# The shared rotary key of the latent attention, projected by four column groups and summed by stacked identities

## The chip, the cores and the metric

The kernel runs on one core of a Trainium2 chip. The metric is the device time of one execution in microseconds; lower is better. Below, TensorE is the matrix engine (PE in the profile; PEld are its weight loads), VectorE is DVE, ScalarE is ACT, GpSimd is POOL, and SyncE (SP) issues most of the large transfers.

## The reference, cut to what matters

Two layers of a transformer-like block work on 256 latent tokens and 256 context tokens of width 1024. In each layer the normed and modulated rows `h` are multiplied by one wide matrix `w_in`, whose 1952 columns hold the inputs of four groups of mixing heads. Columns 384 to 415 are the rotary key `kr`, 32 numbers for each token, shared by the four heads of the latent attention:

```python
zx = hx @ w_in[layer]
zc = hc @ w_in[layer]
...
_, ckv, kr, _, bk, bv, _, dk, dv, _ = split_in(z)
k_rope = kr.reshape(B, L, 1, MLA_ROPE)
if ropes is not None:
    k_rope = apply_rope(k_rope, rope_a)
ka = jnp.concatenate([k_nope, jnp.broadcast_to(k_rope, (B, L, MLA_HEADS, MLA_ROPE))], axis=-1)
```

The rotation is applied to the latent tokens alone. After mixing, each layer runs a mixture of 16 experts. Everything is float32.

## The kernel before, in words

Each engine has its own instruction list, written out by hand and joined by semaphores (`mark` counts one up, `at` gives the value to wait for). Activations lie transposed in `hT`, as 8 slices of 128 rows of the width by 512 tokens (256 latent, then 256 context).

**Projection (`project`, TensorE, L508 to L569).** The columns of `w_in` come in four chunks, loaded by SyncE into three staging buffers. The tiles are made in the order `cq0`, `cq1`, `ckv`, `kr`; `bk`, `bv`, `bq0`, `bq1`; `dq0`, `dk0`, `dq1`, `dk1`; `dv0`, `dv1`, `u0`, `u1`. A tile is a sum over the 8 slices of the width, that is 8 matmuls into one PSUM bank. `take` hands out six banks in a ring and waits until what last lay in the bank was read. For `kr` each of the 8 matmuls has 32 output partitions (64 to 95 of the bank). In layer 1 the first chunk is done differently: `cq0` and `cq1` for the latent tokens, then the transposes that make the context half of `hT`, then `ckv` and `kr` for tokens 0 to 255 and `ckv` and `kr` for tokens 256 to 511, with 256 columns to a matmul. Behind `bk` stand the sums of squares of `cq` (`square_part`, L482), behind `bq1` those of `ckv`. In layer 0, behind the second, third and fourth chunk, a piece of the modulation product stands (`ada_item`, L496): 8 matmuls of 32 output partitions, over four column groups of TensorE.

**What reads the tiles (ScalarE, `project`, L1096 on).** ScalarE copies the tiles out of PSUM in the same order: `cq0`, `cq1`, their squares, `ckv`, `kr` (32 rows, L1106, into `kr[64:96]` in the buffer `lat`), `bk`, then the inverse norm of `cq`, and so on. In layer 0 it first issues the constants' load and small weights' loads (`rest_of_loads`, L1345 on).

**The rotation.** `rotate` (L571) multiplies the copied tile by a matrix that swaps and negates halves. For `kr` this uses 32 rows and 32 columns of `rot_mla`. GpSimd multiplies the tile by the cosines, VectorE the rotated one by the sines, adds both (`rope`), and copies the result to the four heads' keys (L1449). The rotations are the first step after the projection (`latent_projections`, L579), with a wait there for the constants.

`va`, the values of the latent attention, has a buffer of 128 x 1024 in `W[0]` that stays unused until the end of `latent_projections`.

Of the kernel before, what the change touches and what calls it, by code (L numbers as in the profile page):

```python
# [23 lines left out]
P = 128  # L24
D = 1024
KD = D // P
SEQ = 256
# [31 lines left out]
def constants():  # L59
# [45 lines left out]
    put("inv_count", inv_count.reshape(P, -1))  # L105

# [58 lines left out]
def hybrid_block(nc, A, out, known=None):  # L165
    ctx = ExitStack()
    with ctx:
# [54 lines left out]
        qas, kas, bqs, bks, dqs, dks, vas, bvs, dvs, dgs = places.values()  # L222

# [235 lines left out]
        def _(pe):  # L459
# [48 lines left out]
            def project(L):  # L508
                S, nq = f"pe_in{L}", q_tokens(L)

                def tile(name, w, t, lo, hi):

                    col, _ = TILES[name]
                    m, p0 = (MLA_ROPE, MLA_NOPE) if name == "kr" else (P, 0)
                    for k in range(KD):
                        if name in ("cq0", "ckv"):
                            for s in range(lo // SEQ, hi // SEQ):
                                pe.wait_ge(*at("h", L, s, k))
                        if name in ("bq0", "bq1"):

                            for b in range(2):
                                c0 = b * P + int(name[2]) * 64
                                mm = nc.tensor.matmul(t[64 * b:64 * b + 64, lo:hi], w[:, k, c0:c0 + 64], hT[:, k, lo:hi],  # L523
                                                      start=(k == 0), stop=(k == KD - 1), skip_group_check=True)
                        else:
                            mm = nc.tensor.matmul(t[p0:p0 + m, lo:hi], w[:, k, col:col + m], hT[:, k, lo:hi],  # L526
                                                  start=(k == 0), stop=(k == KD - 1))
                    return mm

                for c, names in enumerate((("cq0", "cq1", "ckv", "kr"), ("bk", "bv", "bq0", "bq1"),  # L530
# [17 lines left out]
                    for name in names:  # L548
# [15 lines left out]
                        if name == "bk":  # L564
                            for j in range(2):
                                square_part(S, ("cq", L), j, 2, sq[j][:, 0:nq])
# [3 lines left out]
            def rotate(S, L, name, x, kind, lo, hi):  # L570
# [3 lines left out]
                r = C("rot_" + kind)  # L574
                nc.tensor.matmul(t[lo:hi, 0:SEQ], r[lo:hi, lo:hi], x, start=True, stop=True)\  # L575
                    .then_inc(*mark(S, ("filled", "rot", L, name)))
# [457 lines left out]
        def _(act):  # L1034
# [61 lines left out]
            def project(L):  # L1096
# [9 lines left out]
                copy(S, kr[64:96, :], ("kr", L), lo=64, hi=96, keys=[("tile", L, "kr")])  # L1106
                copy(S, bks[L], ("bk", L), keys=[("tile", L, "bk")])
                finish_rstd(S, ("cq", L), 1, (0, nq), 256, ("ckvn", L - 1) if L else None)
# [1085 lines left out]
```

## Time and profile before

| | us |
|---|---|
| median of 3 executions | 1181.54 (1181.15 to 1188.02) |
| the profiled execution | 1180.66 |
| its span, first to last instruction | 1178.8 |
| TensorE busy | 989.8 (84%) |
| VectorE, ScalarE, GpSimd busy | 314.3, 264.3, 189.6 |
| projection of layer 0 | 34 to about 140 |
| experts of layer 0 | about 430 to 660 |
| projection of layer 1 | 700 to 797 |
| experts of layer 1 | about 930 to 1166 |

Times are counted from the first instruction. An engine's list is worked through in order; a timeline's bracket gives the idle time ahead of a row and what ended it. Each fp32 matmul stands as two records (`x16` is 8 matmuls), and its weight load as two. The weight load of a pass is done while the pass before it runs, so the distance between starts of weight loads gives the pace. The chain of waits is followed back from the last instruction of the kernel.

### The profile page before, as it was taken

The numbers are of one execution on the slowest core, as the hardware profiler recorded it, in microseconds if no ns is written. First come the engines' busy times: TensorE is split into PE (matmuls) and PEld (weight loads), VectorE is DVE, ScalarE is ACT, GpSimd is POOL, SyncE is SP. The second block draws the span as 40 slices with busy tenths as digits, with TensorE's granted clock in tenths as the row PEclk, the third lists the DMA queues.
The fourth block names the chain that finished last, engine by engine and source line by source line (L and its number), as shares of the span: only waits on it lengthen the run. The fifth ranks groups of instructions, "written<-read, shape, count | busy, mean of one in ns | idle before, by whom it ended". The sixth has DMA issues, their size and how long they took to land. (4 is left out here: it accounts for less than half of the span.)

```text
span 1178.8 us, 24765 instructions
## 1 busy us (share of the span) xinstructions
PE 989.8 (84%) x9688; PEld 608.8 (52%) x9689; DVE 314.3 (27%) x876; ACT 264.3 (22%) x708; POOL 189.6 (16%) x312
## 2 busy tenths in 40 slices
PE   3999999999999398987899438999998668798776
PEld 2354646555555365654566235676654444455443
DVE  1100045446632611111111060006562501111112
ACT  4121024445433100100111142114553100000002
POOL 0010015000013211211112110003202222222211
PEclk9999999999999599999999759999999689999899
DMA  9973527765453698999989951320107888999992
GB/s 377 342 223 141 214 90 271 283 241 224 144 232 107 249 377 354 414 424 426 381 335 421 409 207 31 112 72 1 38 1 272 375 353 354 415 414 367 430 428 92
DMA packets 56423, 313.64 MB, mean 266 GB/s; under 512 B 12282, under 2 KB 20516, under 8 KB 37796
## 3 DMA queue, kind: packets, MB, share of 16 engines
q1 hardware_dynamic: 36480, 280.00, 58.9%
q0 software_dynamic: 7152, 24.58, 6.0%
q10 hardware_dynamic: 12724, 8.11, 2.2%
q8 instruction: 49, 0.80, 0.3%
q14 instruction: 18, 0.15, 0.0%
HBM read 304.21 MB, written 14.75 MB: 271 GB/s over the span
## 5 line engine op out<-in xcount | busy, mean ns | idle before, releaser
L914 PE MATMUL psum<-weights,lat 128*32 128x256 f32 x2688 | 165.5, 399 | 41.5 <-issue 21.7
L914 PEld LDWEIGHTS psum<-weights,lat 128*32 128x32 f32 x2688 | 102.9, 115 | 100.4 <-issue 63.7
L526 PE MATMUL psum<-hT,weights 128*128 128x512 f32 (+3 forms) x384 | 137.3, 518 | 4.7 <-ACT lat L1094 3.2
L526 PEld LDWEIGHTS psum<-hT,weights 128*128 128x128 f32 (+1 forms) x384 | 71.1, 187 | 68.4 <-issue 55.3
L929 PE MATMUL psum<-weights,lat 128*32 128x256 f32 x1344 | 82.2, 382 | 5.4 <-ACT lat L1265 5.3
L1256 ACT ACTIVATE lat<-psum 128x128 f32<-128x128 f32 x64 | 17.7, 277 | 289.3 <-PE psum L914 249.7
L1478 DVE TENSOR_REDUCE st<-psum 128x1 f32<-128x512 f32 (+1 forms) x96 | 55.9, 598 | 72.3 <-PE psum L651 26.2
L688 PE MATMUL psum<-weights,R 128*128 128x64 f32 x480 | 63.3, 271 | 5.5 <-ACT R L1171 4.1
L914 PE MATMUL psum<-hT,lat 128*32 128x256 f32 x672 | 46.3, 419 | 25.2 <-issue 14.3
L1158 ACT ACTIVATE R<-psum,st 128x512 f32<-128x512 f32 (+1 forms) x78 | 48.0, 615 | 83.9 <-DVE st L1478 40.0
L929 PEld LDWEIGHTS psum<-weights,lat 128*32 128x32 f32 x1344 | 51.0, 110 | 29.0 <-issue 9.5
L688 PEld LDWEIGHTS psum<-weights,R 128*128 128x128 f32 x480 | 59.2, 191 | 9.7 <-ACT R L1171 9.0
L770 PE MATMUL psum<-weights,hT 128*128 128x512 f32 x144 | 63.5, 595 | 0.2 <-ACT hT L1195 0.2
L1717 DVE STREAM_TRANSPOSE lat<-psum 128x256 f32<-128x256 f32 x25 | 11.3, 450 | 190.0 <-PE psum L853 186.5
L1724 DVE STREAM_TRANSPOSE lat<-lat 128x256 f32<-128x256 f32 x41 | 18.3, 446 | 145.9 <-PE psum L914 140.4
L2007 POOL TENSOR_SCALAR x_tok<-x_tok 128x256 f32<-128x256 f32 x23 | 28.3, 1232 | 166.4 <-PE psum L899 166.0
L1094 ACT ACTIVATE weights<-psum 128x512 f32<-128x512 f32 (+4 forms) x40 | 22.1, 552 | 128.6 <-PE psum L526 55.2
L914 PEld LDWEIGHTS psum<-hT,lat 128*32 128x32 f32 x672 | 25.4, 118 | 43.3 <-issue 36.4
L496 PE MATMUL psum<-weights,silu_c 128*32 128x512 f32 x384 | 46.0, 598 | 1.3 <-DMA weights<-in_ada_w_dram 1.3
L2041 POOL DMA_INDIRECT lat<-h_rows,slot_col x42 | 41.2, 981 | 33.1 <-POOL slot_col L2038 32.3
L1886 POOL TENSOR_TENSOR R<-weights,cst 128x256 f32<-128x256 f32 (+1 forms) x22 | 14.9, 676 | 181.4 <-DVE lat L1435 138.5
L914 PE MATMUL psum<-R,lat 128*32 128x256 f32 x672 | 42.6, 391 | 1.6 <-DMA R<-in_exp_w_gu_dram 1.6
(290 smaller groups left out, 1299.9 us busy)
## 6 DMA issues: line engine op xcount, KB each, us to landing
weights<-in_exp_w_gu_dram SPq DMA_DIRECT2D x44, 2048.0 KB, 12.0
weights<-in_ada_w_dram SPq DMA_DIRECT2D x24, 2048.0 KB, 7.8
weights<-in_exp_w_down_dram SPq DMA_DIRECT2D x22, 2048.0 KB
hT<-in_exp_w_gu_dram SPq DMA_DIRECT2D x10, 2048.0 KB
R<-in_exp_w_gu_dram SPq DMA_DIRECT2D x10, 2048.0 KB
spare_w<-in_exp_w_down_dram SPq DMA_DIRECT2D x10, 2048.0 KB
weights<-in_w_in_dram SPq DMA_DIRECT2D x6, 2048.0 KB, 24.2
weights<-in_w_out_dram SPq DMA_DIRECT2D x4, 2048.0 KB, 8.1
```

The source lines that it names most:

```text
L496: mm = nc.tensor.matmul(psum[32 * g:32 * g + 32, B_ADA, :], silu_c[:, k, :], w[:, k2, g, :], start=(k == 0), stop=(k == 7), skip_group_che ...
L526: mm = nc.tensor.matmul(t[p0:p0 + m, lo:hi], w[:, k, col:col + m], hT[:, k, lo:hi], start=(k == 0), stop=(k == KD - 1))
L688: mm = nc.tensor.matmul(t[:, 0:64], probT[u % 2][:, i, :], v, start=(i == 0), stop=(i == n - 1))
L770: nc.tensor.matmul(t, mixT[:, k, tt * P:(tt + 1) * P], w[:, k, :], start=(k == 0), stop=False)
L914: mm = nc.tensor.matmul(gu_ps[BLK * j:BLK * j + BLK, 0:256], (xgT if L < LAST else xgT_last)[:, k, :], w[:, k % 4, j, :, :], start=(k == 0 ...
L929: mm = nc.tensor.matmul(y_ps[BLK * j:BLK * j + BLK, 0:256], actT[:, b, :], w_dn[place][:, b, j * 256:(j + 1) * 256], start=(b == 0), stop= ...
L1094: a(dst, src, ACT.Copy, scale=scale).then_inc(*mark(S, ("read", *job), *keys))
L1158: a((prob[u % (AHEAD + 1)] if v == 0 else prob2)[:, 0:nk], read(act, "s", L, u, v)[:, 0:nk], ACT.Exp, bias=s_[:, v:v + 1], accum_out=s_[:, ...
L1478: ins = red(s_[:, j:j + 1], read(v, "s", L, u, j)[:, 0:nk], AX.X, ALU.max, negate=True)
L1724: nc.vector.transpose(xgT[:, :, :].rearrange("p k s -> p (k s)"), xg[par]).then_inc(x_ready, 1)
L2007: nc.gpsimd.tensor_scalar(hot, tokens, pair_col[:, 0:1], pair_col[:, 1:2], ALU.is_equal, ALU.mult).then_inc(sem("hot_ready"), 1)
L2041: g_.indirect_dma_start(xg[par], None, h_parts, bass.IndirectOffsetOnAxis(ap=slot_col[:, par:par + 1], axis=0))\
```

## The change

`kr`'s eight matmuls go to four groups of 32 output partitions: slice k of the width to group k mod 4, so that each group sums two slices. The four partial tiles fill all 128 partitions of the bank. ScalarE copies them whole into `kr_parts`, which lies in the unused buffer of `va`. A new step `sum_kr` on TensorE, behind `bk`, multiplies them by four stacked 32x32 identities, which adds the four parts; its result goes to partitions 64 to 95 of another bank, and a second copy of ScalarE, behind that of `bk`, brings it to where the key lay before. The rotation reads the partial tiles, with the rotation stacked four times. The constants grow by two matrices of 32 columns.

```diff
+    put("sum_kr", np.tile(np.eye(MLA_ROPE), (QUADS, 1)))
+    put("sum_rot_kr", np.tile(rot_kr, (QUADS, 1)))
...
+        kr_parts = vas[0].rearrange("p t c -> p (t c)")[:, 0:NTOK]
...
+                        elif name == "kr":
+
+                            p0 = MLA_ROPE * (k % 4)
+                            mm = nc.tensor.matmul(t[p0:p0 + MLA_ROPE, lo:hi], w[:, k, col:col + MLA_ROPE], hT[:, k, lo:hi],
+                                                  start=(k < 4), stop=(k >= 4), skip_group_check=True)
...
+                def sum_kr():
+
+                    pe.wait_ge(*at("const"))
+                    t = take("kr_sum", L)
+                    pe.wait_ge(*at("read", "kr", L))
+                    nc.tensor.matmul(t[MLA_NOPE:MLA_QK, :], C("sum_kr"), kr_parts, start=True, stop=True).then_inc(*mark(S, ("filled", "kr_sum", L)))
...
                         if name == "bk":
+                            sum_kr()
                             for j in range(2):
...
+                if name == "kr":
+                    mm = nc.tensor.matmul(t[lo:hi, 0:SEQ], C("sum_rot_kr"), kr_parts[:, 0:SEQ], start=True, stop=True)
...
-                copy(S, kr[64:96, :], ("kr", L), lo=64, hi=96, keys=[("tile", L, "kr")])
+                copy(S, kr_parts, ("kr", L))
                 copy(S, bks[L], ("bk", L), keys=[("tile", L, "bk")])
+                copy(S, kr[64:96, :], ("kr_sum", L), lo=64, hi=96, keys=[("tile", L, "kr")])
```

TensorE, layer 0, from `kr` to `bv`. Names stand for buffers: `hT` the activations, `weights` the staged matrix or the mixing buffers, `spare_w` the squares; in brackets the semaphores waited for (`act_in0` counts ScalarE's copies of this projection). Before:

```order
L526 MATMUL psum<-hT,weights 32x512 [waits act_start]
L526 MATMUL psum<-hT,weights 32x512 x7
L526 MATMUL psum<-hT,weights 128x512 [waits v_start,dma_stage4]
L526 MATMUL psum<-hT,weights 128x512 x7
L482 MATMUL psum<-spare_w,ones 128x512 [waits act_in0] x2
L556 MATMUL psum<-weights,hT 128x128 [waits v_start]
```

And of the change:

```order
L534 MATMUL psum<-hT,weights 32x512 [waits act_start]
L534 MATMUL psum<-hT,weights 32x512 x7
L537 MATMUL psum<-hT,weights 128x512 [waits v_start,dma_stage4]
L537 MATMUL psum<-hT,weights 128x512 x7
L546 MATMUL psum<-weights,cst 32x512 [waits act_in0,v_start,dma_const]
L489 MATMUL psum<-spare_w,ones 128x512 [waits act_in0] x2
L574 MATMUL psum<-weights,hT 128x128 [waits act_in0]
```

The eight matmuls of `kr` keep their place and number. Between `bk` and the squares stands the product with the identities, with waits for a copy of ScalarE and for the constants; the first matmul of `bv` behind them waits for one of ScalarE's copies too.

ScalarE, layer 0, from the last small loads to the copy of the squares' sum (L1050 before, L1072 in the change). Before:

```order
L1358 DMA subln<-in_diff_subln_dram 128x64
L1094 ACTIVATE lat<-psum 128x512 [waits pe_in0] x2
L1042 ACTIVATE spare_w<-lat 128x512 [waits act_in0] x2
L1094 ACTIVATE lat<-psum 128x512 [waits pe_in0]
L1094 ACTIVATE lat<-psum 32x512 [waits pe_in0]
L1094 ACTIVATE weights<-psum 128x512 [waits pe_in0]
L1050 ACTIVATE spare_w<-psum,cst 128x512 [waits pe_in0]
```

And of the change:

```order
L1381 DMA subln<-in_diff_subln_dram 128x64
L1116 ACTIVATE lat<-psum 128x512 [waits pe_in0] x2
L1064 ACTIVATE spare_w<-lat 128x512 [waits act_in0] x2
L1116 ACTIVATE lat<-psum 128x512 [waits pe_in0]
L1116 ACTIVATE weights<-psum 128x512 [waits pe_in0] x2
L1116 ACTIVATE lat<-psum 32x512 [waits pe_in0]
L1072 ACTIVATE spare_w<-psum,cst 128x512 [waits pe_in0]
```

The 32-row copy into `lat` has moved behind the copy of `bk`, and a full copy of the partial tiles stands where it was.

## Rows read from the trace of the kernel before

**Rows 1.** The page: busy time of each engine, share of the span, instructions.
```profile
PE 989.8 (84%) x9688; PEld 608.8 (52%) x9689; DVE 314.3 (27%) x876; ACT 264.3 (22%) x708; POOL 189.6 (16%) x312
```

**Rows 2.** Timeline of TensorE, layer 0: start, length, line, out<-in, count, idle before.
```profile
33.99 36.45 PE L526 MATMUL psum<-hT,weights 128*128 128x512 f32 x80 [1.52 <-DVE hT L1855]
...
95.94 14.32 PE L526 MATMUL psum<-hT,weights 128*128 128x512 f32 x33
```

**Rows 3.** Chain of waits, layer 1: start, length, what.
```profile
716.36 23.23 PE psum L526 x80
...
797.08 2.04 PE psum L575 x8
```

**Rows 4.** Timeline of TensorE's weight loads around the key, layer 0, columns as above.
```profile
56.32 0.14 PEld L526 LDWEIGHTS psum<-hT,weights 128*32 128x32 f32 x2 [0.76 <-issue]
...
57.21 0.11 PEld L526 LDWEIGHTS psum<-hT,weights 128*32 128x32 f32 x1 [0.32 <-issue]
57.64 0.11 PEld L526 LDWEIGHTS psum<-hT,weights 128*32 128x32 f32 x1 [0.32 <-issue]
...
63.31 0.30 PEld L526 LDWEIGHTS psum<-hT,weights 128*128 128x128 f32 x2 [0.84 <-issue]
```

**Rows 5.** The same view around the key's two halves, layer 1.
```profile
716.33 5.00 PEld L526 LDWEIGHTS psum<-hT,weights 128*128 128x128 f32 x16 [3.39 <-ACT lat L1094]
721.67 3.16 PEld L526 LDWEIGHTS psum<-hT,weights 128*32 128x32 f32 x16 [0.33 <-issue]
725.24 3.32 PEld L526 LDWEIGHTS psum<-hT,weights 128*128 128x128 f32 x16 [0.41 <-issue]
728.89 3.16 PEld L526 LDWEIGHTS psum<-hT,weights 128*32 128x32 f32 x16 [0.33 <-issue]
732.46 0.30 PEld L526 LDWEIGHTS psum<-hT,weights 128*128 128x128 f32 x2 [0.41 <-issue]
```

**Rows 6.** Windows: length, busy of PE, PEld, DVE, ACT, POOL, granted clock, DMA share, GB/s.
```profile
60.00:65.00 5.00, 5.00 (x12) 1.53 (x11) 0.00 (x0) 3.19 (x6) 0.00 (x0) 1.00 0.25 39
443.00:650.00 207.00, 177.08 (x3116) 118.36 (x3111) 35.72 (x99) 21.49 (x66) 38.29 (x66) 0.99 0.96 394
718.00:720.00 2.00, 2.00 (x6) 1.56 (x6) 0.00 (x0) 0.00 (x0) 0.00 (x0) 0.55 0.00 0
720.00:722.00 2.00, 2.00 (x11) 1.41 (x10) 0.00 (x0) 0.00 (x0) 0.00 (x0) 1.00 0.00 0
```

**Rows 7.** Timeline of weight loads around a modulation piece in four column groups.
```profile
93.12 0.16 PEld L496 LDWEIGHTS psum<-weights,silu_c 128*32 128x32 f32 x8 [0.81 <-issue]
...
94.97 0.30 PEld L482 LDWEIGHTS psum<-spare_w,ones 128*128 128x128 f32 x2 [0.84 <-issue]
```

**Rows 8.** Chain of waits, an expert's first product in four column groups.
```profile
937.59 3.59 PE psum L914 x64
```

**Rows 9.** Timeline of weight loads around the key's rotation, layer 1.
```profile
797.01 0.13 PEld L575 LDWEIGHTS psum<-lat,cst 32*32 32x32 f32 x2 [0.33 <-issue]
797.55 1.16 PEld L575 LDWEIGHTS psum<-weights,cst 128*128 128x128 f32 x6 [0.41 <-ACT up L1127]
```

**Rows 10.** Timeline of ScalarE and of its queue (ACTq), layer 0.
```profile
43.92 11.49 ACTq L455 DMA_DIRECT2D w_pool<-in_pool_w_dram  x4
...
60.66 1.08 ACT L1094 ACTIVATE lat<-psum 128x512 f32<-128x512 f32 x2 [23.48 <-issue]
...
63.42 0.59 ACT L1094 ACTIVATE lat<-psum 32x512 f32<-32x512 f32 x1 [0.15 <-PE psum L526]
70.48 0.60 ACT L1094 ACTIVATE weights<-psum 128x512 f32<-128x512 f32 x1 [6.48 <-PE psum L526]
```

**Rows 11.** Issues of DMA at 5.29, 33.28 and 63.41 us: KB, us to landing.
```profile
weights<-in_w_in_dram SPq DMA_DIRECT2D x1, 2048.0 KB, 38.6
cst<-in_constants_dram ACTq DMA_DIRECT2D x1, 1631.5 KB, 10.5
weights<-in_w_in_dram SPq DMA_DIRECT2D x1, 2048.0 KB, 7.9
```

More of the change, by code:

```diff
@@ L105, in constants @@
     put("inv_count", inv_count.reshape(P, -1))
+    rot_kr = rot(MLA_ROPE, MLA_NOPE, MLA_QK)[MLA_NOPE:MLA_QK, MLA_NOPE:MLA_QK]
+    put("sum_kr", np.tile(np.eye(MLA_ROPE), (QUADS, 1)))
+    put("sum_rot_kr", np.tile(rot_kr, (QUADS, 1)))
     put("before", np.triu(np.ones((P, P)), 1) - 1.0)
@@ L513, in tile @@
                     col, _ = TILES[name]
-                    m, p0 = (MLA_ROPE, MLA_NOPE) if name == "kr" else (P, 0)
                     for k in range(KD):
@@ L524, in tile @@
                                                       start=(k == 0), stop=(k == KD - 1), skip_group_check=True)
+                        elif name == "kr":
+                            p0 = MLA_ROPE * (k % 4)
+                            mm = nc.tensor.matmul(t[p0:p0 + MLA_ROPE, lo:hi], w[:, k, col:col + MLA_ROPE], hT[:, k, lo:hi],
+                                                  start=(k < 4), stop=(k >= 4), skip_group_check=True)
                         else:
-                            mm = nc.tensor.matmul(t[p0:p0 + m, lo:hi], w[:, k, col:col + m], hT[:, k, lo:hi],
+                            mm = nc.tensor.matmul(t[:, lo:hi], w[:, k, col:col + P], hT[:, k, lo:hi],
                                                   start=(k == 0), stop=(k == KD - 1))
                     return mm
+                def sum_kr():
[3 more added lines that the diff above has]
+                    nc.tensor.matmul(t[MLA_NOPE:MLA_QK, :], C("sum_kr"), kr_parts, start=True, stop=True).then_inc(*mark(S, ("filled", "kr_sum", L)))
                 for c, names in enumerate((("cq0", "cq1", "ckv", "kr"), ("bk", "bv", "bq0", "bq1"),
@@ L573, in rotate @@
                 t = take("rot", L, name)
-                r = C("rot_" + kind)
-                nc.tensor.matmul(t[lo:hi, 0:SEQ], r[lo:hi, lo:hi], x, start=True, stop=True)\
-                    .then_inc(*mark(S, ("filled", "rot", L, name)))
+                if name == "kr":
+                    mm = nc.tensor.matmul(t[lo:hi, 0:SEQ], C("sum_rot_kr"), kr_parts[:, 0:SEQ], start=True, stop=True)
+                else:
+                    r = C("rot_" + kind)
+                    mm = nc.tensor.matmul(t[lo:hi, 0:SEQ], r[lo:hi, lo:hi], x, start=True, stop=True)
+                mm.then_inc(*mark(S, ("filled", "rot", L, name)))
             def latent_projections(L):
```

## The prediction

> **What bounds the kernel now.** I read the page first, then the granted clock, the chain of waits, and the timelines of each engine around the two places where the rotary key is projected. The page [rows 1] shows TensorE busy for 989.8 us, 84% of the span of 1178.8 us. The execution's own time is 1180.66 us, so 1.9 us lie outside the span. The question is whether TensorE sets the pace just where the change sits. It does in both layers. In layer 0 the timeline of TensorE [rows 2] runs from 33.99 us to 110 us; its seven rows, of which the first and the last stand there, have an idle entry at the first alone. In layer 1 the chain of waits [rows 3] is TensorE's own work from 716.36 us on, through the whole projection to the rotations (L575, 797.08 us): nine rows, of which the first and the last stand there. Nothing else ends last there, so each microsecond taken off TensorE in the projection comes off the span, unless something not timed by TensorE then ends later.
>
> **What is removed.** In layer 0 the key takes 8 matmuls of 32 output partitions by 512 tokens. Each fp32 matmul has two records. The rows of the weight loads [rows 4] show its 16 passes: the first load starts at 56.32 us, the first load of the tile behind it (`bk`) at 63.31 us, so the piece costs 63.31 - 56.32 = 6.99 us. Sixteen passes at the spacing of 0.43 us (57.21 to 57.64 us) are 6.86 us; 0.13 us is what going into and out of the narrow shape costs. In layer 1 the key is made in two halves of 256 tokens, 16 passes each: 721.67 to 725.24 us and 728.89 to 732.46 us [rows 5], 3.57 us each, 7.14 us together. Removed in all: 14.13 us. The granted clock is 1.00 where layer 1's first half begins [rows 6], the level of 2.4 GHz, and 512 columns in 0.43 us in layer 0 are the same pace as 16 passes of 256 in 3.57 us, so these prices are full-speed ones.
>
> **What takes its place.** The eight slices of the width now go to four column groups of 32 output partitions, two slices to each. The trace has this very shape: a piece of the modulation product (L496, 128*32, 512 columns, 8 matmuls over four groups, also all into one bank). Its first load is at 93.12 us and the next line's at 94.97 us [rows 7]: 1.85 us for 16 passes, against 6.99 us for the same number now. That is four passes of 0.43 us plus the same 0.13 us. For 256 columns the nearest row is the expert product (L914), 64 passes in 3.59 us [rows 8], so 16 passes in 0.90 us; with the entry and exit cost 0.13 us I take 1.0 us for each half. New: 1.85 + 2 x 1.0 = 3.85 us. Saved: 14.13 - 3.85 = 10.3 us.
>
> **What is added.** One matmul with the stacked identities per layer (512 columns, 32 output partitions, so two passes of 0.43 us) plus 0.13 us for entering and leaving the shape: 1.0 us. The trace's nearest row is the rotation of this key, one 256-column matmul between wide ones: 797.01 to 797.55 us [rows 9], 0.54 us, which is 0.43 us of passes and 0.11 us besides, so the estimate holds for that as well. Two layers: 2.0 us. The rotation itself keeps its columns and only contracts over 128 rows instead of 32; the passes are counted in columns (16 passes of `ckv`, 128 output partitions, start 3.65 us before the key's next ones, which take 3.57 us with 32 [rows 5]), so I take zero. The sum: -10.3 + 2.0 = **-8.3 us**.
>
> **What is added elsewhere, at nothing.** ScalarE copies a full 128x512 tile instead of 32x512 (0.60 and 0.59 us [rows 10]), and has one more copy of 0.6 us per layer. It idles 6.48 us before the `bk` copy [rows 10], and behind it waits for the square sums, two matmuls of 0.86 us; the new copy (about 66.3 to 66.9 us in the shifted layer 0) fits before these are ready at about 68 us. Without that cover it would cost 0.6 us a layer, 1.2 us. The constants grow by 64 columns, 32 KB on a 1631.5 KB load: 0.08 us at 394 GB/s [rows 6]. They land at 33.28 + 10.5 = 43.8 us [rows 11], long before the sum's matmul at about 65 us. More takes from the bank ring make later tiles wait for newer reads, but in the order only `bv`'s first matmul gets such a wait, for a copy (`cq0`) done by 61.7 us [rows 10].
>
> **What must come earlier with TensorE.** `bk` would start at 58.2 us instead of 63.3. Its weights were issued at 5.29 us and took 38.6 us: 43.9 us [rows 11]. The last chunk is issued when the first is used (63.41 us, landing 7.9 us later [rows 11]), so it moves along. The same holds for the modulation weights and expert weights further on: they are issued as TensorE releases buffers. The DMA queues are nearly saturated in the experts, at a share of 0.96 over 207 us [rows 6], but that stretch starts relative to TensorE too.
>
> **The tightest new wait.** Queued behind the sum's matmul on TensorE are the square sums, then `bv` and all else. It waits for ScalarE's copy of the four partial tiles. ScalarE cannot begin its projection copies before 60.66 us, as it is issuing small loads until then [rows 10]. Then come two copies, two squares and the `ckv` copy; it was free for the key at 63.42 - 0.15 = 63.27 us, so the partial tiles are copied by 63.9 us. TensorE finishes `bk` at about 65.1 us (ScalarE's copy of it began at 70.48 us, so it ended at about 70.3 us, less 5.1). The margin is 1.2 us. In layer 1 it is over 6 us: the partial tiles are full at about 727.3 us and `bk` lasts seven more.
>
> **Rivals.**
> 1. *The wait on ScalarE decides* (the one that ends slower). ScalarE's issues once took long: four small loads 11.49 us, to 55.4 us [rows 10], while weight loads filled the DMA queues; the ten behind them took 5.2 us. The last weight chunk is now issued at 58.3 us, inside ScalarE's last issues. Were these stretched by x, TensorE would stall x - 1.2 us; beyond x = 9.5 us the gain is gone, and a repeat of 11.49 us gives a stall of 10.3 us and 1183.5 us. Against it: the transfer needs a while to flow (before, it was issued at 63.41 us and the DMA share of 60 to 65 us is 0.25 [rows 6, 11]), by which time ScalarE is done. 3 in 100. The Trainium skill (TensorEngine Tiling (Array Packing), Performance Considerations) warns of this kind of bound: tiling speeds up TensorE but not the copies out of PSUM. By that rule ScalarE would set the pace here; the rows of this stretch show it idle before each copy instead.
> 2. *The column groups overlap less well.* If the groups reading the same activations did not overlap at all, nothing is saved and 2.0 us is added: 1183.5 us. L496 and L914 speak against it [rows 7, 8], both with all groups reading the same partitions. 3 in 100. The Trainium skill (TensorE: Matmul & The Clock Gate, Part 3) gives 2.38x measured for three column groups and 3.07x for four row groups, less than the 3.8x that 6.99 / 1.85 makes here; by 3.07x the new piece would be 14.13 / 3.07 = 4.6 us and the sum -7.5 us. The sum above goes by the trace.
> 3. *The clock's slow stretches fall otherwise.* After TensorE's pause before 716.33 us (3.39 us) the clock is at 0.55 in 718 to 720 us, mostly its level of 1.2 GHz, and at 1.00 behind that; those first 16 passes take 5.34 us instead of the 3.65 of the next wide ones [rows 5, 6]: 1.7 us. All work behind shifts by 4 to 8 us, and the experts have many pauses. One such stretch more or less is 1.7 us; two or three more in one direction make 1178 or 1168 us. 12 in 100 for a result over 3.5 us off the sum, either side.
>
> **How the numbers follow.** The profiled execution predicts 1180.66 - 8.3 = 1172.4 us. It lay 0.9 us below the median of 1181.54 us, so the median should be 1181.54 - 8.3 = **1173.2 us**. The forecast has 82 in 100, in 1170 to 1177 us. Rivals 1 and 2 at 1183.5 us together have 6. A range of 1168.5 to 1179 us takes in the clock cases and a partly stretched ScalarE, and leaves out about 1 in 10. A measurement of this kernel can tell about 1% (11.8 us) from no change. Faster by more than that needs a time under 1169.7 us, beyond the 10.3 us removed without any new cost: 6 in 100, by clock stretches only. Slower by over 1% (above 1193 us) needs a stall beyond rival 1's price: 2 in 100. Within 1%: 92.
>
> **What the new profile would show.** Right: weight loads of the key's matmuls in a burst of about 1.85 us in layer 0 and 1.0 us twice in layer 1; `bk` loads starting near 58.2 us; a 128*32 matmul from the constants of about 0.9 us behind `bk`, with no idle time in front; every later row of layer 0 up to the experts about 4.1 us earlier, the second layer's end about 8.3. Wrong: an idle entry of TensorE at the sum, released by ScalarE; key passes spaced by 0.43 us; or an offset between the traces that shrinks in the experts.

## The result, and the profile of the changed kernel

The changed kernel took 1172.68 us (median of 7 executions, 1168.27 to 1176.79), the kernel before 1184.85 us (7, 1181.15 to 1188.02). The ratio is 0.9901, with a 95% interval of 0.9875 to 0.9928: 11.7 us less, 8.5 to 14.8. (Here and below the times are medians. The ratio is worked out from all executions and is not that of the medians; a difference is the ratio times the median of the kernel before.) The forecast was 1173.2 us and 8.3 us less. The time lay in the range. The difference was larger than forecast, and the first question is whether the missing 3.4 us belong to the change.

The profiled execution took 1168.27 us. Its page, in the parts that answer to [rows 1] and to the clock:

```profile
span 1166.4 us, 24777 instructions
PE 975.9 (84%) x9692; PEld 604.2 (52%) x9693; DVE 313.7 (27%) x876; ACT 266.0 (23%) x710; POOL 189.6 (16%) x312
PEclk9999999989999699999999859999999689999988
q8 instruction: 49, 0.80, 0.3%
```

TensorE is busy for 13.9 us less than in [rows 1], at the same share of the span, with four records more (two passes of the sum in each layer). ScalarE has two more instructions and 1.7 us more work. The mean granted clock is 0.947, against 0.941 before. The last line, packets that bring instructions, looked like nothing at first. It matters below.

The timeline of TensorE's weight loads, layer 0 and then layer 1, columns as in [rows 4]:

```profile
54.78 0.16 PEld L534 LDWEIGHTS psum<-hT,weights 128*32 128x32 f32 x8 [0.76 <-issue]
55.23 0.13 PEld L534 LDWEIGHTS psum<-hT,weights 128*32 128x32 f32 x4 [0.30 <-issue]
55.66 0.13 PEld L534 LDWEIGHTS psum<-hT,weights 128*32 128x32 f32 x4 [0.30 <-issue]
56.63 0.30 PEld L537 LDWEIGHTS psum<-hT,weights 128*128 128x128 f32 x2 [0.84 <-issue]
...
717.28 0.59 PEld L534 LDWEIGHTS psum<-hT,weights 128*32 128x32 f32 x16 [0.33 <-issue]
718.28 3.32 PEld L537 LDWEIGHTS psum<-hT,weights 128*128 128x128 f32 x16 [0.41 <-issue]
721.93 0.59 PEld L534 LDWEIGHTS psum<-hT,weights 128*32 128x32 f32 x16 [0.33 <-issue]
722.93 0.30 PEld L537 LDWEIGHTS psum<-hT,weights 128*128 128x128 f32 x2 [0.41 <-issue]
...
729.99 0.14 PEld L546 LDWEIGHTS psum<-weights,cst 128*32 128x32 f32 x2 [0.76 <-issue]
730.97 0.73 PEld L489 LDWEIGHTS psum<-spare_w,ones 128*128 128x128 f32 x4 [0.84 <-issue]
```

In layer 0 the key's sixteen passes go from 54.78 us to the next tile's first load at 56.63 us: 1.85 us, where [rows 4] have 6.99. The loads come in three bursts (8, 4 and 4), one for each pass time of 0.43 us. In layer 1 the halves take 718.28 - 717.28 = 1.00 us and 722.93 - 721.93 = 1.00 us, against 3.57 us in [rows 5]. The sum takes 730.97 - 729.99 = 0.98 us. Each of these is the forecast's own figure within 0.02 us.

What was not forecast stands in the timeline of TensorE, layer 0, to be read with [rows 2]:

```profile
34.01 20.84 PE L537 MATMUL psum<-hT,weights 128*128 128x512 f32 x48 [1.52 <-DVE hT L1878]
54.78 1.92 PE L534 MATMUL psum<-hT,weights 128*32 128x512 f32 x16
56.63 7.13 PE L537 MATMUL psum<-hT,weights 128*128 128x512 f32 x16
64.78 1.02 PE L546 MATMUL psum<-weights,cst 128*32 128x512 f32 x2 [1.02 <-ACT weights L1116]
65.73 1.98 PE L489 MATMUL psum<-spare_w,ones 128*128 128x512 f32 x4
```

and in ScalarE's timeline, the rows that answer to [rows 10]:

```profile
43.99 11.55 ACTq L462 DMA_DIRECT2D w_pool<-in_pool_w_dram  x4
...
58.29 0.68 ACTq L1381 DMA_DIRECT2D rt_b<-in_router_gb_dram  x1
...
61.55 1.08 ACT L1116 ACTIVATE lat<-psum 128x512 f32<-128x512 f32 x2 [24.34 <-issue]
...
64.03 1.09 ACT L1116 ACTIVATE weights<-psum 128x512 f32<-128x512 f32 x2
```

TensorE stands still for 1.02 us ahead of the sum, released by ScalarE's copy (L1116). That is rival 1 on a small scale, and it works against the change. The first of the two copies in the last row is that of the partial tiles. ScalarE starts its copies at 61.55 us instead of 60.66, and TensorE gets to the sum at 64.78 - 1.02 = 63.76 us instead of the forecast 65.1.

So the gain beyond the forecast came from elsewhere. The table sets the start of the same weight loads, issued by SyncE as TensorE releases their buffers, beside each other in both traces:

| issue (place) | before | after | difference |
|---|---|---|---|
| fourth chunk of the projection, layer 0 | 63.41 | 56.77 | -6.64 |
| first modulation weights behind it | 95.10 | 90.66 | -4.44 |
| output projection, layer 0 | 297.61 | 296.33 | -1.28 |
| first projection chunk, layer 1 | 645.37 | 641.13 | -4.24 |
| fourth chunk, layer 1 | 732.56 | 723.06 | -9.50 |
| first expert weights, layer 1 | 890.21 | 881.88 | -8.33 |
| span | 1178.8 | 1166.4 | -12.4 |

Where the change sits the steps are as forecast: layer 1 gains 5.26 us between the fourth and fifth rows (5.14 forecast), then gives back the sum. In layer 0 the -6.64 us is 5.14 us of the change and 1.5 us of an earlier start. Elsewhere the difference wanders over stretches that the change doesn't touch: by 3.2 us between the second and third rows, by 3.0 us between the third and fourth, and by 4.1 us behind the last issue. The windows view says why; the columns are those of [rows 6], first the kernel before and then the changed one:

```profile
34.00:38.00 4.00, 4.00 (x6) 1.84 (x7) 1.81 (x6) 3.18 (x7) 0.00 (x0) 0.61 1.07 405
250.00:265.00 15.00, 14.89 (x93) 8.05 (x92) 6.46 (x29) 5.58 (x22) 1.72 (x3) 1.00 0.74 274
```

```profile
34.00:38.00 4.00, 3.99 (x10) 1.85 (x11) 1.83 (x6) 3.21 (x7) 0.00 (x0) 1.00 1.09 410
250.00:265.00 15.00, 15.00 (x69) 7.94 (x69) 6.58 (x26) 4.60 (x16) 1.72 (x3) 0.77 0.72 249
```

At 34 to 38 us the kernel before ran partly at the level of 1.2 GHz (0.61), the changed one at 2.4 GHz (1.00): 4 x 0.39 = 1.6 us gained. At 250 to 265 us it was the other way round: 15 x 0.23 = 3.5 us lost, which is the 3.2 us that went between the second and third rows. Time lost to the lower level can be added up so (TensorE's busy time in a short window, times 1 less the granted clock). In windows of 4 us over the whole span it makes 31.7 us before and 26.3 after. For this pair of executions, then: the forecast's -8.3, the clock's -5.4, the stall's +1.0, and +0.8 for a wait told of below (8.39 us for 7.57), together -11.9 us against -12.4 measured. Whether the clock's part belongs to the change could not be told from one pair of executions; the experiments bear on it.

### The profile page after: what moved, and what is told of

Read it like the earlier page. It is cut to its first block and busy times, and to the rows that moved or that the text cites. A ratio compares the mean times of both kernels' runs of the same rounds, so it can differ in the third digit from the quotient of the medians.

```text
span 1166.4 us, 24777 instructions
## 1 busy us (share of the span) xinstructions
PE 975.9 (84%) x9692; PEld 604.2 (52%) x9693; DVE 313.7 (27%) x876; ACT 266.0 (23%) x710; POOL 189.6 (16%) x312
## 5 line engine op out<-in xcount | busy, mean ns | idle before, releaser
L936 PE MATMUL psum<-weights,lat 128*32 128x256 f32 x2688 | 161.1, 392 | 41.0 <-issue 24.7
L537 PE MATMUL psum<-hT,weights 128*128 128x512 f32 (+1 forms) x336 | 119.4, 514 | 3.5 <-ACT lat L1116 1.9
L537 PEld LDWEIGHTS psum<-hT,weights 128*128 128x128 f32 x336 | 63.7, 191 | 56.8 <-issue 48.8
L951 PE MATMUL psum<-weights,lat 128*32 128x256 f32 x1344 | 82.9, 385 | 6.3 <-ACT lat L1288 6.3
L951 PEld LDWEIGHTS psum<-weights,lat 128*32 128x32 f32 x1344 | 51.1, 111 | 30.8 <-issue 11.1
L1740 DVE STREAM_TRANSPOSE lat<-psum 128x256 f32<-128x256 f32 x25 | 11.3, 450 | 186.1 <-PE psum L875 182.6
L1116 ACT ACTIVATE weights<-psum 128x512 f32<-128x512 f32 (+4 forms) x42 | 23.2, 556 | 122.4 <-PE psum L537 48.7
L792 PEld LDWEIGHTS psum<-weights,hT 128*128 128x128 f32 x144 | 26.8, 190 | 31.4 <-issue 31.1
## 6 DMA issues: line engine op xcount, KB each, us to landing
R<-in_exp_w_gu_dram SPq DMA_DIRECT2D x10, 2048.0 KB, 13.6
```

The source lines that it names most:

```text
L537: mm = nc.tensor.matmul(t[:, lo:hi], w[:, k, col:col + P], hT[:, k, lo:hi], start=(k == 0), stop=(k == KD - 1))
L792: nc.tensor.matmul(t, mixT[:, k, tt * P:(tt + 1) * P], w[:, k, :], start=(k == 0), stop=False)
L936: mm = nc.tensor.matmul(gu_ps[BLK * j:BLK * j + BLK, 0:256], (xgT if L < LAST else xgT_last)[:, k, :], w[:, k % 4, j, :, :], start=(k == 0 ...
L951: mm = nc.tensor.matmul(y_ps[BLK * j:BLK * j + BLK, 0:256], actT[:, b, :], w_dn[place][:, b, j * 256:(j + 1) * 256], start=(b == 0), stop= ...
```

## The experiments

The theory, A: the sum of the prediction holds, everything else is scatter of the clock. Rivals: the change gains more than its passes (by the clock or something further on), or the groups' overlap hangs on the order of the slices.

### The change a second time, and each layer alone

`e4_change_again` is the changed kernel with no edit, to put 8.3 against 11.7 us.

> The change as it is, beside the others on the same chip, to have its ratio to before a second time. Theory A: 0.5 us of luck aside -7.3 us (-8.3 us plus the stall of 1.0 us), ratio 0.9938. Theory B: again about -11.7 us, ratio 0.990.

Measured: 1172.88 us against 1180.81 (24 executions of before), ratio 0.9932 (0.9905 to 0.9960): -8.0 us, -4.7 to -11.2. The changed kernel reads as in the first comparison (1172.68); it was the kernel before that was 4 us quicker. In this trace the clock's loss is 30.3 us, near the 31.7 of before, and the key starts later:

```profile
34.75 22.54 PE L537 MATMUL psum<-hT,weights 128*128 128x512 f32 x48 [2.33 <-ACT hT L1395]
57.22 1.92 PE L534 MATMUL psum<-hT,weights 128*32 128x512 f32 x16
59.07 7.13 PE L537 MATMUL psum<-hT,weights 128*128 128x512 f32 x16
66.14 1.04 PE L546 MATMUL psum<-weights,cst 128*32 128x512 f32 x2
```

With TensorE 2.4 us later at the sum there is no idle entry in front of it. The stall isn't a fixed cost: it is there when TensorE comes early.

`e1_layer0_only` and `e2_layer1_only` keep the new form in one layer and the old one in the other.

```diff
+NEW = (0,)                      # (1,) in the other kernel
...
+                        elif name == "kr" and L not in NEW:
+                            mm = nc.tensor.matmul(t[MLA_NOPE:MLA_QK, lo:hi], w[:, k, col:col + MLA_ROPE], hT[:, k, lo:hi],
+                                                  start=(k == 0), stop=(k == KD - 1))
...
-                            sum_kr()
+                            if L in NEW:
+                                sum_kr()
```

(with the rotation and ScalarE's copies chosen in the same way)

> Only layer 0 has the four column groups and the sum; layer 1 projects the key as before. Theory A (what TensorE saves in each projection reaches the end): 5.1 us saved less 1.0 us for the sum less the stall of 1.0 us that the profile of the change shows ahead of the sum, so -3.1 us against before, and the offset is the same in the experts of both layers. Theory B (a shift of all that follows makes the experts' waits better by some us more): -5 to -7 us. Slow stretches of the clock scatter single executions by some 1.7 us each.

> Only layer 1 has the four column groups and the sum. Theory A: two halves of 2.57 us saved less 1.0 us for the sum and no stall, -4.1 us against before. Theory B: -6 to -9 us, the surplus showing as shorter waits of TensorE in the experts of layer 1.

Measured: layer 0 alone 1179.03 us, ratio 0.9970 (0.9947 to 0.9994), -3.5 us; layer 1 alone 1178.25 us, ratio 0.9980 (0.9960 to 0.9999), -2.4 us. Both intervals (-0.7 to -6.3 and -0.1 to -4.7 us) hold the term of 4.1 us that the sum gives each layer, layer 0's stall taken off or not; neither holds zero, and neither can tell 3.1 from 4.1 us. Theory B, a shift that the experts magnify, is out for layer 1, where it wanted 6 to 9 us; for layer 0, where it wanted 5 to 7, this comparison doesn't exclude it. The two together make -5.9 us, the whole -8.0; the intervals allow them to be the same.

### Does the order of the slices matter?

`e5_groups_in_pairs` gives each column group two slices in succession, where the change goes round the four groups.

```diff
-                            p0 = MLA_ROPE * (k % 4)
+                            p0 = MLA_ROPE * (k // 2)
...
-                                                  start=(k < 4), stop=(k >= 4), skip_group_check=True)
+                                                  start=(k % 2 == 0), stop=(k % 2 == 1), skip_group_check=True)
```

> The change, with slice k of the width going to group k // 2 instead of k mod 4, so that two matmuls in a row go to the same column group; the same eight matmuls and the same sum. Theory A (the groups work side by side because consecutive matmuls go to different groups): neighbours in one group must follow each other, so the eight take five steps of two passes, 4.3 us in layer 0 instead of 1.85 and 2.3 us in each half of layer 1 instead of 1.0: 5.1 us slower than the change. Rival (each group has a queue of its own, and the order does not matter): 1.85 and 1.0 us as in the change, and the same time.

Measured: 1174.57 us against 1180.83 (23 executions), ratio 0.9944 (0.9925 to 0.9963), -6.6 us. The weight loads decide it:

```profile
55.52 0.18 PEld L534 LDWEIGHTS psum<-hT,weights 128*32 128x32 f32 x8 [0.76 <-issue]
55.98 0.15 PEld L534 LDWEIGHTS psum<-hT,weights 128*32 128x32 f32 x4 [0.28 <-issue]
56.41 0.15 PEld L534 LDWEIGHTS psum<-hT,weights 128*32 128x32 f32 x4 [0.28 <-issue]
57.40 0.30 PEld L537 LDWEIGHTS psum<-hT,weights 128*128 128x128 f32 x2 [0.84 <-issue]
```

57.40 - 55.52 = 1.88 us, against 1.85 round the groups; layer 1's halves take 1.02 us each against 1.00. What A expected of this run fell: four passes for one group, one behind another in the program, did not hold up the passes of the other groups. For this shape the order of the slices isn't part of the gain.

### Where the sum stands, and when ScalarE is free

`e3_sum_after_squares` puts the sum behind the square sums:

```diff
                         if name == "bk":
-                            sum_kr()
                             for j in range(2):
                                 square_part(S, ("cq", L), j, 2, sq[j][:, 0:nq])
+                            sum_kr()
```

`e8_small_loads_later` moves ScalarE's ten issues of small loads from ahead of its copies to behind the `bv` copy of layer 0:

```diff
                 copy(S, bvs[L][:, :, :].rearrange("p t c -> p (t c)"), ("bv", L), keys=[("v", L, "swa")])
+                if L == 0:
+                    row_loads()
```

> The change, with the sum's matmul behind the two square sums instead of in front of them. ScalarE's copy of the partial tiles is then done in layer 0 before TensorE comes to the sum, so the idle 1.0 us ahead of it is gone; the square sums run 1 us earlier. Both theories: 1.0 us faster than the change, with no idle entry of TensorE between bk and bv in layer 0. If the stall were not ScalarE's copy but something else in front of the sum, the time stays that of the change.

> The change, with ScalarE's last ten small loads (gate biases, sinks, lambdas, norm gains) issued behind its copy of the values bv in layer 0 instead of ahead of its first copies. If ScalarE's late start is what the sum's matmul waited for, ScalarE's first copy starts near 55.5 us instead of 60.7 to 61.6 us, and TensorE has no idle entry ahead of the sum even where its clock was full from the start: up to 1.0 us faster than the change. If the wait had another cause, the idle entry of 1.0 us stays.

Measured: `e3_sum_after_squares` 1172.31 us, ratio 0.9925 (0.9895 to 0.9954), -8.9 us; `e8_small_loads_later` 1169.60 us, ratio 0.9913 (0.9886 to 0.9939), -10.3 us. The timeline of TensorE in the first:

```profile
56.60 7.13 PE L537 MATMUL psum<-hT,weights 128*128 128x512 f32 x16
63.57 1.88 PE L489 MATMUL psum<-spare_w,ones 128*128 128x512 f32 x4
65.38 1.04 PE L546 MATMUL psum<-weights,cst 128*32 128x512 f32 x2
66.36 7.41 PE L574 MATMUL psum<-weights,hT 128*128 128x128 f32 x64
```

and in the second, with ScalarE's first copy:

```profile
56.75 7.13 PE L537 MATMUL psum<-hT,weights 128*128 128x512 f32 x16
63.81 1.05 PE L546 MATMUL psum<-weights,cst 128*32 128x512 f32 x2
64.79 1.98 PE L489 MATMUL psum<-spare_w,ones 128*128 128x512 f32 x4
...
54.94 1.08 ACT L1116 ACTIVATE lat<-psum 128x512 f32<-128x512 f32 x2 [17.63 <-issue]
```

Neither has an idle entry, though TensorE came as early as in the trace with the stall (56.60 and 56.75 us against 56.63). Behind the sum and the squares, the next work starts at 66.36 us in the first, 67.55 in the changed kernel. So the stall is caused by ScalarE's late start behind its issues, and costs up to 1.0 us; as a change of the time it is below what these intervals resolve, and whether either kernel is better than the change stays open. The traces of `e5_groups_in_pairs`, `e1_layer0_only`, `e7_sum_five_times` and `e9_change_64_empty` (told of below) have idle entries of 0.25, 0.56, 0.58 and 0.59 us at the same place.

### Taking the passes at their price: twice the old, five times the new

`e6_key_twice` is the kernel before with the key projected twice over. `e7_sum_five_times` is the changed kernel with four more sums in each layer.

```diff
-                    for k in range(KD):
+                    for k in (tuple(range(KD)) + tuple(range(KD)) if name == "kr" else range(KD)):
```

```diff
                     pe.wait_ge(*at("read", "kr", L))
+                    for _ in range(4):
+                        nc.tensor.matmul(t[MLA_NOPE:MLA_QK, :], C("sum_kr"), kr_parts, start=True, stop=True)
```

Neither changes the result: the second set of the key's matmuls starts the sum anew, and each of the five sums overwrites the one before.

> The kernel before, with the eight matmuls of the key issued twice (the second set starts the sum anew, so the result is the same). It adds 6.86 us in layer 0 and 2 x 3.43 us in layer 1 to TensorE. Theory A (what TensorE gains or loses in the projection is gained or lost at the end): 13.7 us slower than before, ratio 1.0116. Theory B (a shift is magnified or swallowed by the experts' waits): off by more than 3 us from that.

> The change, with the product with the stacked identities issued five times in each layer instead of once. Theory A (one costs two passes of 0.43 us, entry and exit are paid once): 4 x 0.86 = 3.4 us more a layer, 6.9 us slower than the change, so about 1.2 us faster than before. Rival (each such matmul pays entry and exit or the drain): 4.0 us a layer, 8 us.

Measured: `e6_key_twice` 1187.30 us, ratio 1.0064 (1.0039 to 1.0089), +7.6 us where A had +13.7; `e7_sum_five_times` 1174.96 us, ratio 0.9954 (0.9931 to 0.9977), -5.4 us where A had -1.2. Both lie outside A, and both are quicker than their added passes allow. The passes themselves cost what they should, by the starts of the weight loads: the key twice over takes 56.40 to 70.25 us in layer 0, 13.85 us (6.99 + 16 x 0.43 = 13.87), and the five sums take 65.70 to 70.12 us, 4.42 us (0.98 + 4 x 0.86). Something further on gives back 13.7 - 7.6 = 6.1 us in the first and 5.4 - 1.2 = 4.2 us in the second. These two runs were what A could not explain, and they led to the find below.

### A wait for instructions

The list of waits shows where. What TensorE waits for between 930 and 1000 us, in the kernel before, in the changed one and in `e6_key_twice` (columns: engine, line, what it waited for, us in total, times, longest):

```profile
PE psum L914 <- issue: 12.4, 4, 7.6
```

```profile
PE psum L936 <- issue: 13.4, 4, 8.4
```

```profile
PE psum L914 <- issue: 3.5, 3, 1.3
```

and the timelines of TensorE behind it, in the same order:

```profile
967.73 3.64 PE L914 MATMUL psum<-hT,lat 128*32 128x256 f32 x32 [7.57 <-issue]
```

```profile
950.58 1.15 PE L921 MATMUL psum<-lat,x_tok 32*128 32x256 f32 x16 [0.49 <-ACT lat L1285]
960.12 3.64 PE L936 MATMUL psum<-hT,lat 128*32 128x256 f32 x32 [8.39 <-issue]
```

```profile
978.61 1.93 PE L914 MATMUL psum<-hT,lat 128*32 128x256 f32 x32 [1.33 <-issue]
```

At one place in layer 1's experts TensorE stands for 7.57 us, and 8.39 in the changed kernel, released by nothing that the trace shows as work. (The row of L921 in the changed kernel is the matmul ahead of the pause; it ends at 951.73 us.) Behind the pause its clock is at the lower level: the granted clock of the changed kernel is 0.50 in 960 to 963.5 us, and 32 passes take 3.64 us instead of 1.93. In `e6_key_twice`, which has 96 more instructions ahead of that place, the wait is 1.33 us and the passes are quick: 6.24 + 1.71 = 7.95 us less, 13.7 - 7.95 = 5.8 us, inside the interval of what was measured. In `e7_sum_five_times`, with 32 more instructions than the changed kernel, the wait is 2.10 us and the 32 passes take 3.31 us: against the changed kernel (8.39 - 2.10) + (3.64 - 3.31) = 6.6 us less, and 1.2 + 6.6 = 7.8 us under the kernel before is inside that run's interval (2.7 to 8.1).

What stands at that place in the program is a branch. Each expert's code ends so (L951 in the kernel before, L973 in the changed one):

```python
with pe.If(n_blocks > 1):
    with pe.Fori(start + 1, start + n_blocks) as g:
        gate_up(g, place)
        down(g - 1, place)
        scatter(g - 1)
```

An expert with more than one block of rows runs the inner loop; one with a single block branches past it. Most of the wait lies in that branch: in the changed kernel it lasts from 951.0 to 958.4 us, and register loads follow it up to the matmul. The branch instruction in the view of its line (PEldq is the sequencer that hands TensorE its instructions; count, then shortest, median and longest in ns, first and last start in us), for the changed kernel in all of layer 0's experts, then at the pause, then at the pause in `e9_change_64_empty`, a run told of below:

```profile
L973 PEldq COMPARE_BRANCH  x16: 68/80/220, 412.2 to 659.7; - x16
L973 PEldq COMPARE_BRANCH  x1: 7422/7422/7422, 951.0 to 951.0; - x1
L973 PEldq COMPARE_BRANCH  x1: 699/699/699, 954.7 to 954.7; - x1
```

Of the 32 branches of this line in the changed kernel three take over 0.25 us: 7.42 us at 951.0, 1.66 at 986.2 and 1.57 at 1013.6. All three go past the inner loop (no second block of that expert stands in the timeline), in code that TensorE comes to for the first time in that layer; the later ones of layer 1 take 0.22 us at most.

The weights that the matmul reads (`hT`) had landed 31 to 32 us before its start, an estimate from the bytes that their queue had moved. What comes late is the program: queue q8, 49 packets of 16 KB on the page. In the view of DMA traffic of the changed kernel, one such packet lies between 955.5 and 956.5 us, and none from there to the matmul's start at 960.12 us:

```profile
q8 instruction: 1, 0.02, 5.8%
```

In all fourteen traces, those with the short wait too, the matmul starts 3.1 to 3.2 us behind the end of such a packet (4.0 to 4.4 us behind its start). That is a pattern in time; three kernels test whether the program's place in its packets is the cause. They put instructions that do nothing but raise a semaphore that nobody reads into TensorE's long pause ahead of layer 1, where they cost no time, and so shift which instruction is the first of its block. The pause in the changed kernel's timeline of TensorE:

```profile
693.88 3.65 PE L1006 MATMUL psum<-cst,R 128*128 128x128 f32 x16 [29.66 <-DVE R L1832]
```


```diff
             for L in range(DEPTH):
                 if L:
+                    for _ in range(64):
+                        pe.sem_inc(sem("pad"), 1)
                     pe.wait_ge(*at("banks_out", L - 1))
```

`e9_change_64_empty` is the changed kernel with 64, `e10_before_64_empty` the kernel before with 64, and `e11_key_twice_160_empty` is `e6_key_twice` with 160: with its own 96 that makes 256. If an instruction takes 64 bytes, 256 are one packet of 16 KB, and the boundary lies where it was at first.

> The change, with 64 semaphore increments that nobody waits for added to TensorE's list ahead of layer 1's first transposes, where TensorE sits idle for 30 us. Nothing else is changed. Theory F (at the third expert of layer 1 TensorE waits some 8 us for a block of its own instructions, and where the blocks' borders fall decides it): the borders move by 64 instructions, the idle entry of about 8 us shrinks to 1 to 3 us as in the kernels with the key made twice and the sum made five times, and the kernel is 4 to 6 us faster than the change, ratio to before 0.989. Rival (the short wait of those two kernels is chance or comes from their later start): the entry stays at 8 us and the time is the change's.

> The kernel before, with the same 64 increments and nothing of the change. Theory F: 4 to 6 us faster than before, ratio 0.996, with the idle entry at the third expert of layer 1 at 1 to 3 us instead of 7.6. Rival: no difference, ratio 1.000.

> The kernel before with the key's matmuls issued twice (96 more instructions on TensorE: each fp32 matmul has two weight loads and two products) and 160 empty increments in TensorE's pause ahead of layer 1, 256 more in all, which is one block of 16 KB at 64 bytes each. Theory F: the borders in layer 1's experts fall where they fell before, the idle entry of 7.6 us is back, and the kernel is 13.7 us slower than before, ratio 1.0116, where the key made twice alone was 7.6 us slower. Rival: as the key made twice alone, ratio 1.006.

Measured, against 1182.24 us of before (16 executions), with the difference by the ratio:

| kernel | us | ratio (95%) | difference |
|---|---|---|---|
| `e9_change_64_empty` | 1165.51 | 0.9860 (0.9823 to 0.9896) | -16.5 |
| `e10_before_64_empty` | 1174.98 | 0.9935 (0.9910 to 0.9960) | -7.7 |
| `e11_key_twice_160_empty` | 1193.58 | 1.0115 (1.0070 to 1.0160) | +13.6 |

The timelines of TensorE, in this order:

```profile
957.10 1.93 PE L936 MATMUL psum<-hT,lat 128*32 128x256 f32 x32 [1.47 <-issue]
```

```profile
967.05 1.93 PE L914 MATMUL psum<-hT,lat 128*32 128x256 f32 x32 [1.30 <-issue]
```

```profile
980.30 3.64 PE L914 MATMUL psum<-hT,lat 128*32 128x256 f32 x32 [8.16 <-issue]
```

Sixty-four empty instructions took 7.7 us off the kernel before, where the rows give (7.57 - 1.30) + (3.64 - 1.93) = 7.98 us, and some 8.5 us off the changed one (16.5 - 8.0, from two comparisons; the rows give 8.6). Theory F had said 4 to 6 us; it had counted the wait and not the slow clock behind it. A shift by a whole block brought the wait back, 8.16 us, with a branch of 7.35 us. The time went the same way, +13.6 us where the full price of the key twice over is 13.7, but its interval is wide (8.3 to 18.9 us, and the medians differ by 11.3 us); it is the trace that decides here. So it is shown that the place of instructions in the blocks makes this wait: with 0, 5 or 10 instructions more than the kernel before the wait is 7.6 to 8.4 us, with 42, 64, 74 or 96 more 1.3 to 2.1 us, with 256 more 8.16 us. That it comes of a branch to code that isn't there yet fits the three slow branches above, but no run took the branch away. Nor was it tried apart whether the full DMA engines make the block late (a share of 0.95 to 1.00 in 951 to 960 us of the changed kernel). The Trainium skill (Runtime: NRT & Kernel Launch, Instruction fetch mechanics) says that the instruction memory is refilled in 16 KiB blocks of 256 instructions, and that crossing a boundary is mostly hidden, but that a taken branch to code outside the blocks held has to wait for a fetch. The block's size agrees with these runs, and so does the warning on branches: here one cost 7.4 us.

### All of it together

`e12_best` is the changed kernel with the edits of `e3_sum_after_squares`, `e8_small_loads_later` and `e9_change_64_empty`.

```diff
-                            sum_kr()
                             for j in range(2):
                                 square_part(S, ("cq", L), j, 2, sq[j][:, 0:nq])
+                            sum_kr()
...
+                    for _ in range(64):
+                        pe.sem_inc(sem("pad"), 1)
...
+                if L == 0:
+                    row_loads()
```

> The change with the sum's matmul behind the square sums, ScalarE's ten small loads issued behind its copy of bv, and 64 empty increments on TensorE in the pause ahead of layer 1. If the parts add: -8.3 us of the change without its stall, and 5 us for the borders, -13 us against before, ratio 0.989. If the borders do not matter: -8.3 us, ratio 0.993.

Measured: 1166.91 us, ratio 0.9871 (0.9833 to 0.9909), -15.2 us. That is the time of `e9_change_64_empty` within the intervals, so the two other edits bring nothing that can be measured. The best version is the change with 64 empty instructions: 16.5 us under the kernel before (12.3 to 20.9), about half of it from the change.

## Why the prediction was right, point by point

**What bounds the kernel.** Right. The steps in the table of issues are those of TensorE's passes, in both layers; nothing else ended last at the key.

**Removed and new passes.** Right, each term within 0.02 us: 6.99 us to 1.85, 3.57 to 1.00 twice. The whole-kernel times agree, if with less sharpness (-8.0 us in the second comparison, -3.5 and -2.4 us for the layers alone). Rival 2, groups that overlap less well, is out: 6.99 / 1.85 = 3.8. The working had left open whether groups must alternate; `e5_groups_in_pairs` shows that they need not.

**The sum and the rotation.** Right: 0.98 us in each layer, and 0.86 for each further one. The rotation now contracts over 128 rows, and takes the time that it took over 32 (0.54 us [rows 9]):

```profile
788.65 0.14 PEld L594 LDWEIGHTS psum<-weights,cst 128*32 128x32 f32 x2 [0.33 <-issue]
789.20 0.94 PEld L597 LDWEIGHTS psum<-weights,cst 128*128 128x128 f32 x5 [0.41 <-ACT up L1150]
```

in the timeline of weight loads, 789.20 - 788.65 = 0.55 us.

**The tightest new wait.** The place and the releaser were named rightly, the margin of 1.2 us was mis-sized. It was reckoned for one arrival of TensorE, that of the profiled execution with its clock at 0.61 in 34 to 38 us. With the clock up there, TensorE came 1.34 us earlier (63.76 us for 65.1), and ScalarE's partial copy released the sum 0.88 us later (64.78 for 63.9), as its issues took longer: 1.34 + 0.88 - 1.2 = 1.02 us, the idle entry. The prediction had also answered the bound by the copies with "idle before each copy"; ahead of ScalarE's first copy that idle time (23.48 us [rows 10]) is the time of its issues, and no slack. ScalarE's ten small loads went from 55.58 to 61.55 us, 5.97 us, against 5.2 before. How long they take goes with the start of the weight load of the fourth chunk:

| kernel | chunk issued at | ScalarE's ten issues |
|---|---|---|
| before | 63.41 | 5.21 |
| `e10_before_64_empty` | 62.04 | 5.24 |
| `e2_layer1_only` | 61.93 | 5.24 |
| `e4_change_again` | 59.20 | 5.23 |
| `e7_sum_five_times` | 58.15 | 6.92 |
| `e5_groups_in_pairs` | 57.56 | 5.94 |
| `e9_change_64_empty` | 57.50 | 6.21 |
| `e1_layer0_only` | 56.87 | 5.78 |
| the change | 56.77 | 5.97 |
| `e3_sum_after_squares` | 56.73 | 5.88 |

Where the chunk is issued behind 59 us, they take 5.2 us; where it is issued up to 58.2 us, 0.6 to 1.7 us longer. The two kernels with the key twice over, whose chunk comes at about 70 us, have 5.36 and 5.57 us, so 0.4 us of it can have another cause. That is what rival 1 described, at a tenth of its price. The step of the prediction that failed here is "the transfer needs a while to flow", "by which time ScalarE is done".

**The clock.** Rival 3 was right in kind. No single execution shows the change's size: two executions of the changed kernel differ by 4.0 us in clock loss (26.3 and 30.3), half of what the change is worth. The first comparison's interval (8.5 to 14.8 us) just misses the forecast's 8.3; the second's (4.7 to 11.2) holds it. We read 11.7 us as 8.3 us and scatter, mostly of the kernel before, whose median was 1184.85 us there and 1180.81, 1180.83 and 1182.24 us later. Over all executions on record, a mean granted clock higher by 0.001 goes with 0.60 us less. Set to the same clock, the changed kernel's mean is 8.2 us lower in the second comparison, give or take 2; for the first, the clocks of the kernel before aren't on record. The mean clocks differ little there (0.9426 and 0.9422), so the change doesn't gain by the clock as far as this can tell; it isn't proved.

**What the working missed.** The sum took the rest of the program as rigid. It is not: 96 instructions more, or 64, move the block boundaries on TensorE and with them a wait of 8 us at a branch. The change adds 10 instructions to TensorE's trace, 5 in each layer (two weight loads, two products and a wait), and left the long wait where it was (7.57 and 8.39 us). Had it added 64, the prediction would have missed by 8 us with every term right. Nothing in the prediction guarded against that, and its range held the result without knowing of it. The row was there to be read: the list of waits of the kernel before has a wait of 7.6 us on "issue", where the other three of that line make (12.4 - 7.6) / 3 = 1.6 us each.

## What to carry to other kernels

A matmul with 32 output partitions costs as much as one with 128; spread over four column groups, in either of the two orders tried, it costs a quarter plus some 0.13 us, so long as the sum of the partial results (1 us here) is a small part of what is saved. Where an edit gains less or more than its passes say, look in the waits for a long one on "issue" that comes or goes with the number of instructions, and for a branch at that place that takes microseconds, before looking for a cause in the edit; a few empty instructions in a pause can take it away (here 64 did). A margin read from one execution holds for that execution's clock: reckon it for the earliest arrival as well.

## What the runs showed of the hardware

- The traces list 49 or 50 packets of 16 KB on the instruction queue; that such a block holds 256 of TensorE's instructions agrees with the return of the wait after a shift by 256. At one branch past an inner loop the wait was 7.57 to 8.39 us, where the branch instruction itself lasted 6.7 to 7.5 us, and 1.7 us more went by the lower clock behind it. With 96 more instructions it was 1.33 us at the same matmul.
- The same branch took 0.07 to 0.22 us in the experts of layer 0 (16 times), and 1.57 and 1.66 us at two other places in layer 1 that TensorE came to for the first time.
- Two slices for one column group, one directly behind the other, overlap with those of other groups as well as slices that go round: 1.88 against 1.85 us for 16 passes of 512 columns.
- Going into and out of the narrow shape cost 0.13 us for 512 columns. The Trainium skill (TensorE: Matmul & The Clock Gate, Part 3) gives a speedup of 3.07 for four row groups; here four column groups had 3.8, that cost included.
- ScalarE's ten issues of small loads took 5.2 to 5.6 us with no weight load issued among them (that of `e4_change_again` came at 59.20 us, near their end, and left 5.23), and 5.8 to 6.9 us with one issued by 58.2 us.
